# Block transposes in the first self-attention, an earlier place for ScalarE's weight rounding, and one more weight asked for ahead of the gathers

## The reference

```python
score = where(key_pos <= query_pos, indexer_score, -inf)       # the best 128 keys are kept
s = einsum('qhd,khd->hqk', q, k) * 64 ** -0.5                  # the others get -inf
o = einsum('hqk,khd->qhd', softmax(s, axis=-1), v)
return (o * silu(gate)) @ w_out                                # every block also adds gate * branch
```

## Time and profile before

| | us |
|---|---|
| median of 3 runs (lowest, highest) | 3255.43 (3254.47, 3259.03) |
| the profiled execution | 3252.9 |
| its span, first to last instruction | 3250.9 |
| TensorE busy in the span | 3223.4 |
| mean granted TensorE clock | 0.998 of full |

### The profile page before, as it was taken

One profiled execution on the slowest core, in us unless ns is written; L12 is line 12 of the kernel. 1 busy time (PEld: TensorE's weight loads), 2 busy tenths in 40 slices (PEclk: granted clock), 3 DMA queues, 4 the chain that ended last, 5 costly groups with the idle time before them and its releaser, 6 DMA issues.

```text
span 3250.9 us, 40100 instructions
## 1 busy us (share of the span) xinstructions
PE 3223.4 (99%) x15156; PEld 2547.6 (78%) x15156; DVE 1613.1 (50%) x2736; ACT 1292.0 (40%) x1984; POOL 1570.8 (48%) x1224
## 2 busy tenths in 40 slices
PE   9999999999999999999999999999999999999999
PEld 7788778787877767767788888887676788888887
DVE  4566433546543678864555321227887455442020
ACT  4343643334464322454446322232235544642231
POOL 4554334545434563334463565646333446446473
PEclk9999999999999999999999999999999999999999
DMA  4323224323223523452353433334236235334332
GB/s 158 98 84 97 75 88 147 120 94 92 81 84 91 184 98 101 142 145 81 112 182 98 130 118 97 102 122 139 91 119 166 77 112 187 118 117 123 97 91 97
DMA packets 145976, 370.16 MB, mean 114 GB/s; under 512 B 18670, under 2 KB 35630, under 8 KB 145784
## 3 DMA queue, kind: packets, MB, share of 16 engines
q1 hardware_dynamic: 145784, 367.60, 37.0%
HBM read 316.02 MB, written 25.30 MB: 105 GB/s over the span
## 4 chain that ended last, share of the span: by engine, by line
PE 93%; DVE 4%; ACT 2%; issue 1%; POOL 1%; DMA 0%; SPq 0%; DVEq 0%; ACTq 0%
PE B L942 27%; PE B L944 27%; PE B L943 27%; PE B L1007 1%; PE B L1111 1%; PE B L1134 1%; PE B L1167 1%; PE B L1209 1%; PE B L1217 1%; PE B L1198 1%; POOL WSP L1732 1%; PE B L1082 1%; PE B L1073 1%; PE B L1148 1%; PE B L1203 0%
## 5 line engine op out<-in xcount | busy, mean ns | idle before, releaser
L1732 POOL TENSOR_TENSOR WSP<-WRAW,WSP 128x512 fp32r<-128x512 f32 x1036 | 1359.0, 1333 | 1469.9 <-ACT WSP L1350 1469.4
L942 PE MATMUL B<-H,WSP 128*128 128x512 f32 x2496 | 993.0, 398 | 7.7 <-POOL WSP L1732 7.7
L944 PE MATMUL B<-H,WSP 128*128 128x512 f32 x2496 | 972.6, 390 | 0.0
L943 PE MATMUL B<-H,WSP 128*128 128x512 f32 x2496 | 971.9, 389 | 0.0
L1350 ACT ACTIVATE WSP<-WRAW 128x1024 fp32r<-128x1024 f32 (+1 forms) x567 | 555.8, 984 | 669.3 <-PE B L944 528.7
L942 PEld LDWEIGHTS B<-H,WSP 128*128 128x128 f32 x2496 | 468.8, 188 | 127.6 <-issue 25.3
L943 PEld LDWEIGHTS B<-H,WSP 128*128 128x128 f32 x2496 | 469.0, 188 | 100.9 <-issue 6.9
L944 PEld LDWEIGHTS B<-H,WSP 128*128 128x128 f32 x2496 | 468.5, 188 | 99.0
L1815 DVE TENSOR_TENSOR B<-B,RN 128x512 f32<-128x512 f32 x194 | 134.8, 697 | 392.1 <-PE B L944 375.8
L942 PE MATMUL B<-YM,WSP 128*128 128x512 f32 x512 | 199.5, 390 | 0.0
L944 PE MATMUL B<-YM,WSP 128*128 128x512 f32 x512 | 199.2, 389 | 0.0
(11 more groups left out here) (451 smaller groups left out, 4806.8 us busy)
## 6 DMA issues: line engine op xcount, KB each, us to landing
WRAW<-in_wb SPq DMA_DIRECT2D x318, 512.0 KB, 3.7
WRAW<-in_wa SPq DMA_DIRECT2D x153, 512.0 KB, 3.7
PTB<-BLK SPq DMA_DIRECT2D x128, 128.0 KB, 2.7
WRAW<-in_wa SPq DMA_DIRECT2D x50, 256.0 KB, 2.6
WRAW<-in_wb SPq DMA_DIRECT2D x48, 256.0 KB, 2.6
parked<-HYT SPq DMA_DIRECT2D x24, 256.0 KB, 2.1
QA<-RXA SPq DMA_DIRECT2D x64, 64.0 KB, 2.0
xs<-PA SPq DMA_DIRECT2D x16, 256.0 KB, 4.4
```

The source lines that it names most:

```text
L942: e.matmul(o, L[0], R[0], start=first, stop=False)
L943: e.matmul(o, L[0], R[1], start=False, stop=False)
L944: return e.matmul(o, L[1], R[0], start=False, stop=last)
L1732: x = e.tensor_tensor(WSP[:, i % NSP, 1, c:c + CUT], WRAW[:, i % NRAW, c:c + CUT], WSP[:, i % NSP, 0, c:c + CUT].bitcast(fp32), ALU.subtract)
```

## The change

- In the first self-attention VectorE adds the mask within PSUM, ScalarE's exponential reads PSUM there and writes into `PA` in an order of keys that a transpose of 32x32 blocks can use. `score_bank` gives the scores four banks in turn. Unit `tr` is gone on all engines. New are `ablocks` (VectorE turns 32x32 blocks in place) and `agather` (SyncE, eight DMAs per half of the queries). `pv` reads each half by itself: 12 products per `c`. `PA` has six tiles, `PTA` six; the parts of `PA` above the causal edge are set to zero once per layer.
- The order of units of the attention is new, and so are the pick strings of both layers.
- ScalarE rounds piece `w0 + 3` right behind the unit of piece `w0` rather than at the start of the next one with a weight.
- SyncE asks for one piece more before it waits for the blocks of a gather, in both attentions.

The diff, where the pick string of the other layer and some context are left out, and each part is moved to the left:

```diff
@@ -21,13 +21,13 @@
 PICKS = {
     "one0": (
...
-        "1211211222112211120001102121112222011121211112212212100000200000000000020002002000002000000000000020"
-        "020000000200000200020002000002000"
+        "1211211222112211120001100212111222201112121111221221210000000000000020000200000000000000000000200002"
+        "00000000000000200202020000000000002222000"
...
@@ -434,21 +434,27 @@
-main += qk(0)
+def sc(c, i):
+    return Unit("sc", "a", l, c, i, s=True)
+
+def nrm(c, i):
+    return Unit("nrm", "a", l, c, i)
+
+def turned(c, i):
+    return Unit("ablocks", l, c, i)
+
+nxt = qk(1)
+main += qk(0) + [sc(0, 0), *nxt[:2], nrm(0, 0), sc(0, 1), *nxt[2:4], turned(0, 0), nrm(0, 1), sc(0, 2), *nxt[4:], turned(0, 1),
+                 Unit("agather", l, 0, 0), nrm(0, 2), sc(0, 3), turned(0, 2), nrm(0, 3), turned(0, 3), Unit("agather", l, 0, 1)]
 for c in range(4):
-    nxt = qk(c + 1) if c < 3 else []
-    for i in range(4):
-        main.append(Unit("sc", "a", l, c, i, s=True))
-        main += nxt[:2]
-        nxt = nxt[2:]
-        if i:
-            main.append(Unit("tr", "a", l, c, i - 1, t=True))
-        main.append(Unit("nrm", "a", l, c, i))
-    main += nxt
-    main.append(proj("agate", l, c, src=H, w=[(*A, "agate", c)]))
-    main.append(Unit("tr", "a", l, c, 3, t=True))
-    main.append(Unit("pv", "a", l, c, o=True))
-    main += [Unit("atty", l, c), Unit("split", "YB", A, c)]
+    nxt = qk(c + 2) if c < 2 else []
+    if c:
+        main += [Unit("agather", l, c, 0), sc(c, 2), sc(c, 3), nrm(c, 2), turned(c, 2), nrm(c, 3), turned(c, 3),
+                 Unit("agather", l, c, 1)]
+    main += nxt[:2] + [proj("agate", l, c, src=H, w=[(*A, "agate", c)])]
+    if c < 3:
+        main += [sc(c + 1, 0), sc(c + 1, 1), nrm(c + 1, 0), nrm(c + 1, 1), *nxt[2:], turned(c + 1, 0), turned(c + 1, 1)]
+    main += [Unit("pv", "a", l, c, o=True), Unit("atty", l, c), Unit("split", "YB", A, c)]
 if n:
@@ -677,7 +683,7 @@
 BIAS, VA4, QA, KA = at(34, "BIAS", 3), at(37, "VA4", 4), at(41, "QA", 2), at(43, "KA", 2)
-PA, PTA, RXA, GA = at(45, "PA", 4), at(49, "PTA", 8), at(57, "RXA", 4), at(62, "GA", 3)
+PA, PTA, RXA, GA = at(45, "PA", 6), at(51, "PTA", 6), at(57, "RXA", 4), at(62, "GA", 3)
@@ -901,7 +907,16 @@
-    return (S0, S1)[hh] if ab == "a" else (S0, S1, T0, T1)[(2 * i + hh) % 4]
+    return (S0, S1, T0, T1)[(2 * i + hh) % 4]
+
+def query_half(t, h, hh):
+
+    return t[:, 2 + 2 * hh:4 + 2 * hh, :].rearrange("p s x -> p (s x)") if h else t[:, hh, :]
+
+def weights_tile(i, hh):
+
+    t = query_half(PA, i // 2, hh).rearrange("p (b j i k) -> p i b j k", b=4, i=2, k=32)
+    return t[:, i % 2, :, 0:i + 1, :]
@@ -1103,20 +1118,12 @@
         if ab == "a":
-            b = take((S0, S1)[hh], dve_done, ("smax", ab, l, c, i, hh))
+            b = take(score_bank(ab, i, hh), act_done, ("exp", ab, l, c, i, hh))
             q, kk = QA[half, c % 2, 128 * i:128 * i + 128], KA[half, c % 2, 0:n]
...
         e.matmul(b[:, 0:n], q, kk, start=True, stop=True).then_inc(*mm_done.up(("sc", ab, l, c, i, hh)))
-elif k == "tr":
-    ab, l, c, i = a
-    nk = i + 1
-    for hh in range(2):
-        b = take((T0, T1)[hh], (dve_done, act_done)[hh], ("pt", ab, l, c, i, hh))
-        w.wait_ge(act_done, ("nrm", ab, l, c, i, hh))
-        p = PA[:, 2 * (i % 2) + hh, :]
-        turn(b, [p[:, 128 * j:128 * j + 128] for j in range(nk)], nk, ("tr", ab, l, c, i, hh))
 elif k == "pbc":
@@ -1138,14 +1145,17 @@
 b = take(O, dve_done, ("lo", "YB", ("a", l), c))
-w.wait_ge(dve_done, ("pt", ab, l, c, 3, 0))
-w.wait_ge(act_done, ("pt", ab, l, c, 3, 1))
+for h in range(2):
+    w.wait_ge(gathered[h], ("agather", l, c, h))
 w.wait_ge(act_done, ("tok", "vtok", l, 3))
-for j in range(4):
-    q0 = 128 * j
-    for hh in range(2):
-        v = VA4[:, j, 128 * c + 64 * hh:128 * c + 64 * hh + 64]
-        x = e.matmul(b[64 * hh:64 * hh + 64, q0:512], v, PTA[:, 4 * hh + j, q0:512], start=j == 0, stop=j == 3)
+for h in range(2):
+    for j in range(2 * h + 2):
+        i0 = max(2 * h, j)
+        for hh in range(2):
+            v = VA4[:, j, 128 * c + 64 * hh:128 * c + 64 * hh + 64]
+            p = query_half(PTA, h, hh).rearrange("p (r j q) -> p j r q", r=4, j=2 * h + 2)[:, j, :, 32 * (i0 - 2 * h):64]
+            o = b[64 * hh:64 * hh + 64, :].rearrange("p (i r q) -> p r i q", i=4, r=4)[:, :, i0:2 * h + 2, :]
+            x = e.matmul(o, v, p, start=j == 0, stop=j == 2 * h + 1)
 x.then_inc(*mm_done.up(("pv", *a)))
@@ -1377,14 +1387,18 @@
 own = [0]
-for u in plan:
+begun = None
+for behind, u in zip([None] + plan, plan):
     k, a = u.kind, u.a
...
         own.append(act_done.n)
+    if behind and behind.w and behind.kind != "woa":
+        next_halves(behind.w0 + len(behind.w) + NSP - 1)
     for g in range(len(u.w)):
-        if u.w0 + g:
+        if g or begun and begun.kind == "woa":
             next_halves(u.w0 + g + NSP - 1)
+    begun = u if u.w else begun
     if k == "nadd":
@@ -1525,16 +1539,19 @@
 ab, l, c, i = a
-n = 128 * (i + 1) if ab == "a" else 512
 m = SM[:, 6 + i, :]
...
 w.wait_ge(dve_done, ("neg", ab, l, c, i))
+if ab == "a" and c:
+    w.wait_ge(gathered[i // 2], ("agather", l, c - 1, i // 2))
 if ab == "b" and (c or i > 1):
...
 for hh in range(2):
-    p = (PA if ab == "a" else PB)[:, 2 * (i % 2) + hh, 0:n]
-    s = p if ab == "a" else banks[score_bank(ab, i, hh)][:, :]
+    p = weights_tile(i, hh) if ab == "a" else PB[:, 2 * (i % 2) + hh, :]
+    s = banks[score_bank(ab, i, hh)][:, :]
+    if ab == "a":
+        s = s[:, 0:128 * (i + 1)].rearrange("p (j k b) -> p b j k", k=32, b=4)
     e.activation(p, s, ACT.Exp, bias=m[:, 2 + hh:3 + hh], scale=SM[:, 4 + c % 2, 2 * i + hh:2 * i + hh + 1],
@@ -1542,21 +1559,11 @@
     ab, l, c, i = a
-    n = 128 * (i + 1)
     w.wait_ge(dve_done, ("rsum", ab, l, c, i))
     for hh in range(2):
-        p = PA[:, 2 * (i % 2) + hh, 0:n]
+        p = weights_tile(i, hh)
         e.activation(p, p, ACT.Copy, scale=SM[:, 6 + i, 6 + hh:7 + hh]).then_inc(
             *act_done.up(("nrm", ab, l, c, i, hh)))
-elif k == "tr":
-    ab, l, c, i = a
-    nk = i + 1
-    if i == 0 and c:
-        w.wait_ge(mm_done, ("pv", ab, l, c - 1))
-    w.wait_ge(mm_done, ("tr", ab, l, c, i, 1))
-    e.activation(PTA[:, 4:4 + nk, 128 * i:128 * i + 128],
-                 banks[T1][:, 0:128 * nk].rearrange("p (k q) -> p k q", q=128), ACT.Copy).then_inc(
-        *act_done.up(("pt", ab, l, c, i, 1)))
 elif k in ("fm1", "fm2"):
@@ -2094,20 +2101,23 @@
 m, q2 = SM[:, 6 + i, :], SM[:, 4 + c % 2, 2 * i:2 * i + 2]
+if (ab, c, i) == ("a", 0, 0):
+    for x in range(8 if l else 0):
+        w.wait_ge(landed, ("xs", 1, x))
+    for h, t in enumerate((PA[:, 0:2, :], PA[:, 2:6, :])):
+        ahead = t.rearrange("p s x -> p (s x)").rearrange("p (n j x) -> p j n x", n=8, j=2 + 2 * h)
+        e.memset(ahead[:, 1 + 2 * h, :, 0:32], 0.0).then_inc(*dve_done.up(("ahead", l, h)))
 if ab == "a":
...
         w.wait_ge(dve_done, ("bias", l, i))
-    if c or i > 1:
-        back = (c, i - 2) if i > 1 else (c - 1, i + 2)
-        w.wait_ge(mm_done, ("tr", ab, l, *back, 1))
 if c and ab == "a":
...
     if ab == "a":
-        x = e.tensor_tensor_reduce(out=PA[:, 2 * (i % 2) + hh, 0:n], in0=b[:, 0:n], in1=bias, scale=1.0, scalar=NEG,
+        x = e.tensor_tensor_reduce(out=b[:, 0:n], in0=b[:, 0:n], in1=bias, scale=1.0, scalar=NEG,
                                    op0=ALU.add, op1=ALU.max, accum_out=m[:, hh:hh + 1])
@@ -2139,15 +2149,12 @@
     e.tensor_copy(wide, m[:, 6:8].unsqueeze(2).to_broadcast([128, 2, 64])).then_inc(*dve_done.up(("share", l, c, i)))
-elif k == "tr":
-    ab, l, c, i = a
-    nk = i + 1
-    if i == 0 and c:
-        w.wait_ge(mm_done, ("pv", ab, l, c - 1))
-    w.wait_ge(mm_done, ("tr", ab, l, c, i, 0))
-    e.tensor_copy(PTA[:, 0:nk, 128 * i:128 * i + 128],
-                  banks[T0][:, 0:128 * nk].rearrange("p (k q) -> p k q", q=128)).then_inc(
-        *dve_done.up(("pt", ab, l, c, i, 0)))
+elif k == "ablocks":
+    l, c, i = a
+    for hh in range(2):
+        p = weights_tile(i, hh)
+        w.wait_ge(act_done, ("nrm", "a", l, c, i, hh))
+        e.transpose(p, p).then_inc(*dve_done.up(("ablocks", l, c, i, hh)))
 elif k == "atty":
@@ -2725,9 +2732,20 @@
         load(G1[:, c, :], parked[l, 12 + c], ("gld", l, 1, c))
+elif k == "agather":
+    l, c, half = a
+    next_raw(coming[n_unit] + NRAW + 1 + half)
+    if half == 0 and c:
+        w.wait_ge(mm_done, ("pv", "a", l, c - 1))
+    w.wait_ge(dve_done, ("ablocks", l, c, 2 * half + 1, 1))
+    for hh in range(2):
+        for q in range(4):
+            n = 128 + 128 * half
+            e.dma_start(query_half(PTA, half, hh)[:, n * q:n * q + n], query_half(PA, half, hh)[32 * q:32 * q + 32]).then_inc(
+                *gathered[half].up((k, *a)))
 elif k == "gather":
     l, c, half = a
-    next_raw(coming[n_unit] + NRAW + half)
+    next_raw(coming[n_unit] + NRAW + 1 + half)
     if half == 0 and c:
```

(4 more changed lines are left out.)

## The result

| | before | after |
|---|---|---|
| median (lowest, highest), us | 3254.95 (3253.15, 3259.03) | 3310.97 (3308.63, 3312.68) |
| ratio to before, with its 95% interval | | 1.017 (1.0152 to 1.0187) |
| span of the profiled execution, us | 3250.9 | 3308.0 |
| mean granted TensorE clock | 0.998 | 0.992 |

The change makes the kernel 56 us slower. Forecast were 28.7 us less, with a range that ended at 3241.

What follows compares the result with a forecast made beforehand. TensorE, busy 3223.4 of 3250.9 us, was taken as the bound. Terms -17.6 - 3.4 - 3.7 + 1.5 - 4.5 - 5.0 + 4.0 = -28.7 us gave a median of 3226.7, 8-in-10 range 3217 to 3241.

Steps and rivals of the forecast that it cites:

- the transposes, the switches and the waits in front of them: First attention, TensorE: 17.6 us for transposes removed, 3.4 for fewer switches to small products, 3.7 for waits before transposes.
- 1.5 back for `pv`: First attention's product with the values: 2.48 us instead of 2.30, eight times, so +1.5 us (0 to +6.4).
- rival 1: Two slow-clock dips in the first attention go with the transposes: 3.4 us lower, 3223.3; chance 0.10.
- TensorE's busy time: A sign that the forecast is right: TensorE busy about 3202 us over the profiled execution.
- the exponential: First attention, ScalarE reading every fourth number of PSUM: no price taken, double time (+0.8 us each) as upper end.
- one rounding (1.04) stands ahead of the last two chunks: Seven hand-overs from residual sum to next norm: early rounding delays the chunks, nothing to 7.3 us.
- the term of +4 us for all new waits: Allowance for all new waits from the early rounding and SyncE's extra piece: +4 us, between 0 and 12.
- ScalarE, VectorE, SyncE in the attention ... are off the path: First attention: these engines' work costs nothing as long as `pv` is reached later than the gather lands.
- the cover of 22 us against 18.5: First attention at `c` = 3: projections of 22.1 us hide the 18.5 us chain to the gather, 3.6 us spare.
- the rounding's own gains: Earlier rounding removes waits: 4.5 us at two of 1.65 and one of 1.17, 5.0 at the memory's keys.
- "Slower": Whole kernel slower by more than 0.2%, 6.5 us: chance 0.05, from rival 4.
- rival 4: SyncE's gathers starve the weights at late halves: +59 us at all eight, +44 at six, 3271; chance 0.05.

Runs made afterwards that it cites:

- r11: r10, with ScalarE rounding the weight three behind the attention's gate projection before that gate's silu; 3223.73 us, ratio 0.9899.
- r9: r7, with SyncE asking for one weight more ahead of the very first gather of layer 0; 3234.29 us, ratio 0.9936.
- r6: The changed kernel, with SyncE asking for one weight further ahead in the output products; 3271.82 us, ratio 1.005.
- r4: All of the change, but ScalarE's early rounding waits behind the residual-sum units (nadd) for the next unit with a weight; 3270.49 us, ratio 1.0042.
- r12: r6, with SyncE's further request also at the second block's keys' and queries' projections; 3261.55 us, ratio 1.0021.
- r1: The kernel before with only the new attention and order of units, rounding and requests as before; 3257.94 us, ratio 1.0003.
- r10: r9, with the unit of the queries' and keys' norms (qss) ahead of the next two scores; 3228.0 us, ratio 0.9913.
- r5: The kernel before with only SyncE's request for one piece more ahead of the second block's gathers; 3254.44 us, ratio 0.9996.
- r3: The kernel before with only ScalarE's early rounding; 3331.6 us, ratio 1.0234.
- r7: All of the change, early rounding only ahead of both attentions' exponentials and scalings, block transposes and the memory's squares; 3237.97 us, ratio 0.9946.
- r8: The kernel before with early rounding only at r7's chosen places, old attention and requests; 3259.44 us, ratio 1.0014.

## Why the prediction was wrong

**Right: the transposes, the switches and the waits in front of them.** The prediction summed them to 24.7 and gave 1.5 back for `pv`, 23.2 net, plus 3.4 if the slow clock goes with them (rival 1). r11, in which only 0.5 us of the attention is late, twice, and the clock never falls there, shows 27.0. This holds for r11, which has another order of units and another rounding; in the change itself the two attentions gained 3.6 and 8.5 us of it. TensorE's busy time, forecast near 3202, is 3200.3 in r9 and 3197.4 in r11, but 3234.7 in the change.

**Right: `pv`.** It was put at 2.48 us instead of 2.30. From its first instruction to the next it takes 2.32 in r11:

```profile
345.42 2.38 PE L1158 MATMUL B<-PTA,VA 128*64 128x256 f32 x24
347.74 1.77 PE L1126 MATMUL B<-KA,QA 64*128 64x384 f32 x8
```

Output in runs of 32 costs nothing, as the earlier trace rows had it. By the rule of the Trainium skill that was weighed there (SBUF — State Buffer, Door 1: The DMA port swizzle) such output slows matmuls significantly. The trace doesn't bear it out for this form, with 2.32 us against 2.30.

**Right: the exponential**, for which no price was taken. Reading every fourth number of PSUM it takes 774 ns, beside 776 in a row:

```profile
L1555 ACT ACTIVATE PA<-B,SM 128x512 f32<-128x512 f32 x16 | 12.3, 774 | 6.9 <-DVE SM L2127 6.2
```

**The step that failed: "one rounding (1.04) stands ahead of the last two chunks"**, 7.3 us at most for seven hand-overs, in the term of +4 us for all new waits. I priced the rounding by its own length. What stands ahead of the chunks is the rounding and its wait: 5.76 us for a weight that is asked for late because SyncE stands for the same chunks. Measured 41 us at six of the seven hand-overs, slow clock included; 39 to 43 by r6 and r4. The prediction had named a wait for HBM as what early rounding "can cost", and gave it +4 with the other new waits; it asked who waits for ScalarE, but not whether SyncE's request for this very weight is behind one of them. That closes the loop.

**The same failure at the second block's norms**: +6.8 and +7.0 us, half of it slow clock behind the wait, and by r12 again the request behind SyncE's transfers. The allowance of 4 us (0 to 12) for all new waits was too small for these two places alone.

**Failed: "ScalarE, VectorE, SyncE in the attention ... are off the path".** I worked out the chain to the gather and held the cover of 22 us against 18.5; that was right. I didn't ask what the denser exponentials do to the rounding behind them. Under the old rounding they cost all of the gain (r1), so the attention's 23 us were never a term of their own.

**Half right: the rounding's own gains**, put at 9.5 us. The two waits of 1.65 us go in all kernels with early rounding (-1.9 us each, so 3.7 in place of the 3.3 priced). That of 1.17 stays where the place isn't chosen (1.18 in r10) and turns into a wait of 2.3 for `ES` where it is early. At the memory's keys the 5.46 us become 1.67, 1.32, 0.93 and 0.47 in r11, 4.4 together: ScalarE's order there has more than one customer. Its slow clock is still there in after, moved along (third row of the next fence).

**Failed: rival 1's dips.** The windows of the earlier trace rows run at full clock in after, but only since the work behind them has moved. The same dips stand further on (windows as before):

```profile
375.00:380.00 5.00, 5.00 (x17) 4.01 (x17) 0.39 (x3) 4.97 (x15) 2.51 (x2) 0.66 0.66 178
925.00:930.00 5.00, 5.00 (x16) 3.92 (x17) 0.33 (x2) 4.97 (x15) 2.19 (x2) 0.67 0.59 167
1620.00:1629.00 9.00, 8.48 (x42) 8.26 (x43) 4.13 (x6) 4.74 (x9) 6.74 (x5) 0.62 0.19 61
```

Ahead of the first two TensorE had neither a transpose nor a wait for over 20 us (the last of both at 348.63 and 898.29), but 24 small products, the last 16 of two columns. Ahead of the first:

```profile
372.50 0.93 PE L1126 MATMUL B<-KA,QA 64*128 64x128 f32 x8
373.36 1.95 PE L1097 MATMUL B<-CST,RXA 128*128 128x2 f32 x16
375.16 0.60 PE L957 MATMUL B<-H,WSP 128*128 128x512 f32 x1
```

That is what the prediction had held against the rival. r4 has the same order of units there and no dip, r9 has one in the first layer and none in the second, and in r10 and r11, where the 16 come ahead of the 8, there is none in either layer. The dips of before are no surer. r5 has the same work as before up to the second block, the two transposes of the earlier trace rows too, and its clock doesn't fall there:

```profile
345.00:350.00 5.00, 5.00 (x33) 4.20 (x30) 1.45 (x7) 4.46 (x11) 0.00 (x0) 1.00 0.38 99
```

So a single trace doesn't tell what such a dip comes from, and the 3.4 us of rival 1 are not a sure part of any of these kernels.

**The chances.** "Slower" stood at 0.05, on rival 4 alone, SyncE's gathers starving the weights. That happens once (r9, 3.7 us), not at six places. The slower side had a second mechanism, and the earlier trace rows pointed to it: ScalarE already waited 67.8 us for raw weights in the longer group and 53.1 in the other, without TensorE waiting for long. In after the two are 104.4 and 109.8, and its waits with no releaser named, such as that of 5.76, went from 17.5 to 86.0.

**Open.** r3 costs 74 us and the change 56, and r7 against r8 is 21.5: the parts don't add up to the microsecond, since each wait removed uncovers another. TensorE's busy time of after is 37 us above that of r11, of which the clock explains 27; the rest isn't traced.

## What to carry to other kernels

When work is moved ahead on an in-order engine, price its wait and not its length, and follow that wait's releaser through the queue that issues it: if the issuing queue waits for anything that stands behind the moved work, there is a loop. The mending is then in the queue: asking one item earlier in SyncE, at two kinds of places, gave back 48 of 56 us. And a part that looks free (an engine busy 40%) can decide another part's gain; test the parts in pairs, as the block transposes and the early rounding each gained nothing alone and 17 us together at chosen places, 32 with one more request, the order of units and one more rounding mended.

## What the runs showed of the hardware

A wait of 3.57 us of TensorE (r1, 367.64) is followed by 5.4 us at a granted clock of 0.50, and in r11, whose longest wait for a weight is 1.8 us, the clock stays at 1.00 to the end of the span. Behind the wait of 3.13 us of after (288.22) it stays at 1.00 too, so a wait of this length doesn't always bring it down. In this kernel a wait of TensorE can cost up to three quarters of its length again in clock: after has 46 us more idle time and loses some 20 more to the clock.

The clock also falls without a wait. 24 small products in 2.66 us (372.50 to 375.16) are followed by a stretch at 0.66 in after, and by a fall in r9 at the same place, with TensorE busy throughout. The rule of the Trainium skill weighed in the prediction (TensorE: Matmul & The Clock Gate, Part 4: PE-mode transpose), by which transposes don't count as work for the clock as other matmuls do, is not what decides here: two dips came with no transpose in the 20 us before them, and r5 has the transposes of the earlier trace rows and no dip. What decides stays open, since the same 24 are followed by no dip in r4.
